# First modulation weight by columns in quarters, low output quarters on GpSimd, an early product in the second quarter of the passes

## The reference, cut to what matters

```python
mod = (silu(c) @ w_mod + b_mod)                    # c: (1, 1024), w_mod: (1024, 6144)
sh1, sc1, g1, sh2, sc2, g2 = split(mod, 6)         # and the same of c_ctx
h  = rms_norm(x, norm1_g) * (1 + sc1) + sh1        # 1024 tokens
hc = rms_norm(ctx, norm1_g) * (1 + csc1) + csh1    # 256 tokens
q_a, k_a, v_a, q_b, k_b, v_b = split(h @ w_in)     # and of hc
o_a, o_b = window_attention(...), neighbourhood_attention(...)
x = x + g1 * (concat(rms_norm(o_a), rms_norm(o_b)) @ w_out)
x = x + g2 * ((silu(h2 @ w_gate) * (h2 @ w_up)) @ w_down)
# second block: y @ w_in_2, a gMLP and a gated linear attention mixer, w_out_2, then
f = square(relu(rms_norm(h, pre_ff_g) @ w_ff1)) @ w_ff2
```

## Time and profile before

| | |
|---|---|
| median of 3 runs | 2323.98 us (2321.5 to 2325.11) |
| profiled execution | 2320.64 us, its span 2318.9 us |
| PE busy | 2263.4 us (98%) |
| PEld busy | 1867.7 us (81%) |
| DVE busy | 1481.0 us (64%) |
| ACT busy | 1020.7 us (44%) |
| POOL busy | 365.6 us (16%) |
| mean granted clock of PE | 0.995 |

### The profile page before, as it was taken

The page is one execution under the profiler, slowest core; times in us unless marked ns, Lnnn a source line. Parts: engine busy times, 40 slices in busy tenths (PEclk is TensorE's granted clock), DMA queues, the critical chain, the costliest instruction groups (busy, mean ns, idle before and its releaser), DMA issues. The chain is left out here.

```text
span 2318.9 us, 34643 instructions
## 1 busy us (share of the span) xinstructions
PE 2263.4 (98%) x12884; PEld 1867.7 (81%) x12884; DVE 1481.0 (64%) x2408; ACT 1020.7 (44%) x2030; POOL 365.6 (16%) x342
## 2 busy tenths in 40 slices
PE   6999999999999999999999999999989999999998
PEld 3878778878878888888888976988878888888886
DVE  3533278776687777776689423234587777666687
ACT  3523178875343232323444433233355555444444
POOL 2493400154340000000001000131240000000011
PEclk9999999999999999999999999999999999999999
DMA  8142350015213232326654411113224444666553
GB/s 321 37 147 90 120 120 28 2 47 167 107 58 124 89 126 86 119 87 214 212 186 142 148 37 46 38 38 143 103 96 150 150 152 148 239 202 217 173 168 123
DMA packets 156129, 289.73 MB, mean 125 GB/s; under 512 B 11998, under 2 KB 59820, under 8 KB 152764
## 3 DMA queue, kind: packets, MB, share of 16 engines
q1 hardware_dynamic: 155964, 287.52, 36.8%
HBM read 219.04 MB, written 70.62 MB: 125 GB/s over the span
## 5 line engine op out<-in xcount | busy, mean ns | idle before, releaser
L2270 PE MATMUL ps<-ff_b_hi,ff_a_hi 128*128 128x512 f32 x448 | 174.5, 390 | 0.2 <-DVE ff_b_lo L2258 0.2
L2271 PE MATMUL ps<-ff_b_lo,ff_a_hi 128*128 128x512 f32 x448 | 174.3, 389 | 0.0
L2272 PE MATMUL ps<-ff_b_hi,ff_a_lo 128*128 128x512 f32 x448 | 174.3, 389 | 0.0
L2231 ACT ACTIVATE ff_a_hi<-ff_a_raw 128x512 fp32r<-128x512 f32 x112 | 70.7, 631 | 157.3 <-PE ps L2272 149.9
L1964 ACT ACTIVATE swiglu_w_hi<-swiglu_stage 128x512 fp32r<-128x512 f32 x110 | 69.0, 630 | 160.6 <-PE ps L2023 151.9
L2021 PE MATMUL ps<-ht_hi,swiglu_w_hi 128*128 128x512 f32 x352 | 137.8, 392 | 0.6 <-DVE ht_lo L1916 0.6
L2022 PE MATMUL ps<-ht_lo,swiglu_w_hi 128*128 128x512 f32 x352 | 137.0, 389 | 0.0
L2023 PE MATMUL ps<-ht_hi,swiglu_w_lo 128*128 128x512 f32 x352 | 137.0, 389 | 0.0
L2256 DVE TENSOR_TENSOR ff_a_lo<-ff_a_raw,ff_a_hi 128x512 fp32r<-128x512 f32 x112 | 80.6, 719 | 83.2 <-ACT ff_a_hi L2231 83.2
L453 DVE TENSOR_TENSOR w_lo<-stage,w_hi 128x2048 fp32r<-128x2048 f32 x23 | 58.9, 2562 | 112.6 <-ACT w_hi L449 112.4
L2270 PE MATMUL ps<-swiglu_b_hi,swiglu_a_hi 128*128 128x512 f32 x308 | 120.3, 391 | 0.4 <-DVE swiglu_b_lo L2258 0.4
(11 more groups left out here) (466 smaller groups left out, 6479.9 us busy)
## 6 DMA issues: line engine op xcount, KB each, us to landing
ff_a_raw<-ff_act_dram SPq DMA_DIRECT2D x112, 256.0 KB, 2.7
swiglu_a_raw<-swiglu_act_dram SPq DMA_DIRECT2D x77, 256.0 KB, 2.8
stage<-w_in SPq DMA_DIRECT2D x18, 1024.0 KB, 5.2
stage<-w_mod SPq DMA_DIRECT2D x16, 1024.0 KB, 4.6
ff_stage<-w_ff SPq DMA_DIRECT2D x16, 1024.0 KB, 5.4
ff_act_dram<-ff_act_sums SPq DMA_DIRECT2D x16, 1024.0 KB, 4.3
ff_act_dram<-ff_acts SPq DMA_DIRECT2D x16, 768.0 KB, 5.6
swiglu_stage<-w_gate SPq DMA_DIRECT2D x11, 1024.0 KB, 6.3
```

The costliest lines, as they stand in the source:

```text
L2231: act.activation(a_hi[r][:, :], a_raw[s % LOOK][:, :], ACT.Copy).then_inc(f.a2_hi, 1)
L2270: pe.matmul(bank, a_hi[r][:, cols], b_hi[r][:, :], start=first, stop=False)
L2271: pe.matmul(bank, a_hi[r][:, cols], b_lo[r][:, :], start=False, stop=False)
L2272: return pe.matmul(bank, a_lo[r][:, cols], b_hi[r][:, :], start=False, stop=last)
```

## The change

1. SP loads the 2048 columns in four quarters by columns (`mod_quarter` on SP): 256 columns of the shift and 256 of the scale, two loads of 1 MiB with pieces of 1 KB, all 1024 rows. Behind quarter 0 come the constants, tiles 0 and 1 and part 0 of `w_in`; then quarter 1, part 1, quarter 2, tiles 2 and 3, quarter 3. PE sums a quarter with 8 matmuls 2x512: rows j and j+4 go to the same one of four partition groups (`mod_quarter_pe`), and four small matmuls with `row_picks` add up and turn the four groups. Each quarter gives the columns of two chunks (`mod_quarter_dve`), from which ACT and DVE make these two chunks (`quarter_hi_of_pair`, `quarter_y_of_pair`, `half_lo_of_pair`). In PE's order the sums of quarters 1 to 3 stand inside the products of the first pair, and the turn of the first pair behind quarter 0.
2. The low quarters of `w_out` in attention are made by POOL (`quarter_low`), at the end of its tables; the last two of the four units in which ACT makes the high quarters move; `rows_a` is cut in two, tiles 0 to 4 ahead of the last `table_inner` and 5 to 7 behind.
3. In both passes the product P1 of the second quarter stands ahead of P4 of the first, with the turn of the last block after its second step, and the turns use the banks differently so that bank 5 is free for it.

The core of the diff (the new functions whole):

```diff
+        def mod_quarter_pe(pe, g):
+
+            pe.wait_ge(modw_in[g], 32)
+            for j in range(KT):
+                at_row = 32 * (j % 4)
+                sums = ps[at_row:at_row + 2, 3, :].rearrange("p (s n) -> p s n", s=2)
+                mm = pe.matmul(sums, cond[:, :, j], mod_w[:, :, j, 256 * g:256 * g + 256], start=(j < 4), stop=(j >= 4))
+            mm.then_inc(part_done, 1)
+            pe.wait_ge(part_evac, g + 1)
+            for e in range(4):
+                pe.matmul(ps[:, 2, 8 * e + 2 * g:8 * e + 2 * g + 2], mod_part[:, e * P:(e + 1) * P], row_picks[:, :],
+                          start=True, stop=True).then_inc(mod_done, 1)
+
+        def mod_quarter_dve(dve, g):
+
+            dve.wait_ge(part_done, g + 1)
+            dve.tensor_copy(mod_part[:, :], ps[:, 3, :]).then_inc(part_evac, 1)
+            dve.wait_ge(mod_done, 4 * g + 4)
+            if g == 0:
+                dve.wait_ge(vec_ready, 1)
+            for w in range(2):
+                dve.tensor_tensor(mod_cols[:, w, :].rearrange("p (s k) -> p s k", s=2)[:, :, 2 * g:2 * g + 2],
+                                  ps[:, 2, 0:32].rearrange("p (s h g w) -> p w g s h", s=2, h=2, w=2)[:, w, g],
+                                  vec_cols[:, 0:16].rearrange("p (s k) -> p s k", s=2)[:, :, 2 * g:2 * g + 2], ALU.add).then_inc(cols_done, 1)
+            dve.wait_ge(cols_done, 3 * g + 2)
+            dve.scalar_tensor_tensor(out=gain_cols[:, :, 2 * g:2 * g + 2], in0=mod_cols[:, :, KT + 2 * g:KT + 2 * g + 2], scalar=1.0,
+                                     in1=bcast(vec_cols[:, 16 + 2 * g:18 + 2 * g], 1, 2), op0=ALU.add, op1=ALU.mult).then_inc(cols_done, 1)
...
+        def quarter_hi_of_pair(act, g):
+
+            act.wait_ge(tr_done, 2)
+            act.wait_ge(cols_done, 3 * g + 3)
+            for k in (2 * g, 2 * g + 1):
+                source, gain, shift = pair_source(0, k)
+                act.activation(pair_tokens(0, 0)[:, k, :], source, ACT.Identity, bias=shift, scale=gain).then_inc(chunk_hi, 1)
...
+        def quarter_y_of_pair(dve, g):
+
+            dve.wait_ge(cols_done, 3 * g + 3)
+            dve.wait_ge(chunk_hi, 2 * g + 2)
+            for k in (2 * g, 2 * g + 1):
+                source, gain, shift = pair_source(0, k)
+                made = dve.tensor_scalar(pair_y(0)[:, k, :], source, gain, shift, ALU.mult, ALU.add)
+            if g % 2:
+                made.then_inc(y_made, 1)
...
+        def half_lo_of_pair(dve, half):
+
+            ks = slice(4 * half, 4 * half + 4)
+            dve.wait_ge(y_made, half + 1)
+            dve.wait_ge(chunk_hi, 4 * half + 4)
+            dve.tensor_tensor(pair_tokens(0, 1)[:, ks, :], pair_y(0)[:, ks, :], pair_tokens(0, 0)[:, ks, :].bitcast(F32),
+                              ALU.subtract).then_inc(tl_done, 1)
...
-                    if i == 0:
-                        pe.wait_ge(w_lo_done, P_X + part + 1)
                     wh, wl = piece_weights(0, part)
                     for k in range(4):
+                        if i == 0 and k % 2 == 0 and 2 * part + k // 2:
+                            mod_quarter_pe(pe, 2 * part + k // 2)
+                        if i == 0 and k == 0:
+                            pe.wait_ge(w_lo_done, P_X + part + 1)
...
-            pair_hi(act, 0)
+            quarter_hi_of_pair(act, 0)
+            quarter_hi_of_pair(act, 1)
             split_hi(act, 1, 1)
+            quarter_hi_of_pair(act, 2)
             sums_of_pair(act, 1)
+            quarter_hi_of_pair(act, 3)
...
-        QUARTER_AT = [unit(B, 2, 3), unit(B, 2, 5), unit(B, 2, 7), unit(B, 3, 0)]
+        QUARTER_AT = [unit(B, 2, 3), unit(B, 2, 5), unit(B, 3, 0), unit(B, 3, 1)]
...
-                if u in QUARTER_AT:
-                    quarter_dve(dve, QUARTER_AT.index(u))
...
-                    rows_a(pool)
+                    roots_a(pool)
+                    rows_a(pool, range(5))
                 for j in range(2):
                     table_inner(pool, i, j)
+            rows_a(pool, range(5, NT))
+            for q in range(4):
+                quarter_low(pool, q)
...
-        def quarter_dve(dve, q):
+        def quarter_low(pool, q):
 
             if q == 3:
-                dve.wait_ge(w_hi_done, P_O + 1)
+                pool.wait_ge(w_hi_done, P_O + 1)
             else:
-                dve.wait_ge(quarter_hi, q + 1)
-            low = dve.tensor_tensor(quarter(out_lo0, q), quarter(out_raw, q), quarter(out_hi0, q).bitcast(F32), ALU.subtract)
+                pool.wait_ge(quarter_hi, q + 1)
+            low = pool.tensor_tensor(quarter(out_lo0, q), quarter(out_raw, q), quarter(out_hi0, q).bitcast(F32), ALU.subtract)
             if q == 3:
                 low.then_inc(w_lo_done, 1)
...
+                dve.wait_ge(w_lo_done, P_O + 1)
...
+            def mod_quarter(g):
+                for side in range(2):
+                    first = D * side + 256 * g
+                    sp.dma_start(mod_w[:, side, :, 256 * g:256 * g + 256],
+                                 t["w_mod"][0].rearrange("(p k) n -> p k n", k=KT)[:, :, first:first + 256]).then_inc(modw_in[g], 16)
+
+            def x_rows(first):
+                for j in (first, first + 1):
+                    sp.dma_start(q_nat[:, j, :], t["x"][0, j * P:(j + 1) * P, :]).then_inc(x_in[j], 16)
+
+            mod_quarter(0)
+            sp.dma_start(ident[:, :], t["k_ident"]).then_inc(pe_consts_in, 16)
+            sp.dma_start(vec_rows[0:16, :], t["b_mod"][0, 0:2 * D].rearrange("(k n) -> k n", n=P)).then_inc(vec_in, 16)
+            sp.dma_start(vec_rows[16:24, :], t["norm1_g"][0].rearrange("(k n) -> k n", n=P)).then_inc(vec_in, 16)
+            x_rows(0)
+            load_weights(sp, P_X, x_piece(0, 0), in_piece(stage))
+            mod_quarter(1)
             load_weights(sp, P_X + 1, x_piece(0, 1))
+            mod_quarter(2)
+            x_rows(2)
+            mod_quarter(3)
...
+            pe.transpose(ps[:, 2, 32:56], vec_rows[0:24, :], ident[0:24, 0:24]).then_inc(vec_turned, 1)
+            mod_quarter_pe(pe, 0)
+            pair_turn(pe, 0, q_nat[:, 0:2, :])
             first_pe(pe)
...
+            dve.memset(ps[:, 3, :], 0.0).then_inc(banks_clear, 1)
+            dve.wait_ge(pe_consts_in, 16)
+            dve.tensor_reduce(row_picks[:, :], ident[:, :].rearrange("p (g r) -> p r g", r=32)[:, 0:2, :], AX_X, ALU.add).then_inc(banks_clear, 1)
...
+            dve.tensor_copy(vec_cols[:, :], ps[:, 2, 32:56]).then_inc(vec_ready, 1)
+            dve.wait_ge(banks_clear, 2)
+            mod_quarter_dve(dve, 0)
             for b in range(2):
                 root_tile(dve, b, T_X, q_nat[:, b, :])
+            quarter_y_of_pair(dve, 0)
             split_lo(dve, 0, 0)
...
+            mod_quarter_dve(dve, 1)
+            quarter_y_of_pair(dve, 1)
+            half_lo_of_pair(dve, 0)
+            split_lo(dve, 1, 1)
+            mod_quarter_dve(dve, 2)
+            quarter_y_of_pair(dve, 2)
+            for b in (2, 3):
+                root_tile(dve, b, T_X, q_nat[:, b, :])
+            mod_quarter_dve(dve, 3)
+            quarter_y_of_pair(dve, 3)
+            half_lo_of_pair(dve, 1)
...
-                return 4 + (e % 4 if e < 12 else (e - 12) % 3)
+                return 4 + (e % 4 if e < 12 else (0, 1, 2, 0, 2, 0, 2, 0)[e - 12])
...
+            def made_at(q, b):
+                return {(0, P4): 7, (1, P1): 6}.get((q, b), place_of(q, b))
...
-                    pe.wait_ge(f.lo7, f0.lo7 + 24)
+                    pe.wait_ge(f.lo7, f0.lo7 + (18 if b == P1 else 24))
...
-            f.turn_block(pe, 4, 3)
+            for k in f.product_steps(pe, 1, P1):
+                if k == 1:
+                    f.turn_block(pe, 4, 3)
             f.product(pe, 0, P4)
-            for q in range(1, f.Q):
+            for b in range(1, 7):
+                f.product(pe, 1, b)
+            for q in range(2, f.Q):
                 for b in range(7):
...
             f.weight_lo(dve, 0, P4)
+            f.weight_lo(dve, 1, P1)
             f.block_lo(dve, 4, 0)
-            f.weight_lo(dve, 1, P1)
```

More of the change, by code:

```diff
@@ L182, in program @@
         y_made, chunk_hi = early("y_made"), early("chunk_hi")
-        modw_in = [early(f"modw_in{j}") for j in range(8)]
+        modw_in = [early(f"modw_in{j}") for j in range(4)]
         ctx_landed = early("ctx_landed")
@@ L1455, in rows_a @@
             pool.wait_ge(on_in, 32)
-            for j in range(NT):
+        def rows_a(pool, tiles):
+            for j in tiles:
                 row = q_nat[:, j, 0:AW]
@@ L2034, in keep @@
             def keep(act, q):
[L2036 removed]
+                act.wait_ge(f.made, f0.made + made_at(q, P1) + 1)
                 if q:
```

62 lines of the change are left out of this document (9 added, 53 removed).

## The result

| | before | changed |
|---|---|---|
| median | 2324.95 us (7 runs, 2320.9 to 2331.94) | 2330.34 us (7 runs, 2326.81 to 2339.77) |
| span of the profiled execution | 2318.9 us | 2328.0 us |
| PE's mean granted clock | 0.995 | 0.993 |

The ratio is 1.0040, 95% interval 1.0025 to 1.0055: the changed kernel is slower by 0.4%, some 9 us. (The two medians lie only 5.4 us apart, the profiled executions 9.1. The forecast was 2324.6, a change of +0.6 us, with "within 0.2%" as the likeliest; the measured time lies inside the range, on the side of rival 1.

A forecast was written before the change was run, and what follows sets the result against it. TensorE, busy 98% of the span, was taken as the bound, leaving only 55.5 us idle or lower-clock time to change. Startup 7.5, attention −3.5 and passes −3.4 gave +0.6 on 2323.98: 2324.6 us, 8-in-10 range 2317 to 2331.5.

The forecast's parts named there:

- rival 1: Startup: half clock through all quarters, sums as well as products; startup +14.9, net +8.0, 2332 us; chance 0.27.
- part A: Startup with w_mod in quarters: more turnarounds and late low weights eat the earlier start; +7.5 us, between +5.5 and +9.6.
- a shift passes through whole: After the startup: TensorE work is a chain, so any shift of the second pair's first product reaches the end whole.
- part C: Both passes: an early product of 2.76 us covers PE's waits of 1.7 and 2.0; −3.4, bounds −2.5 and −3.7.
- Part B: Attention: low quarters moved from DVE to GpSimd remove PE's waits for `small`; −3.5 us, bounds −1.5 and −3.8.
- it would be wrong if: Signs: quarter 1 or 2 sums wait for loads, early products wait for weights, or time after 60 us changes elsewhere.
- The chain: Startup: three later quarters of 6.93 us each after the first product, second pair at 56.6 at upper clock, +5.5 us.
- Quarter 0: Startup: data there at 11, sums to 14.7, first product at 25.7 us, 10.3 earlier than before.
- The clock, where I chose: Startup turnarounds: +5.5 us if the upper clock holds, +9.6 if it falls in each; the middle, +7.5, was taken.
- The sign that I had named: Startup, 25 to 58 us: mean granted clock about 1.00 at +5.5, about 0.75 at +9.6, below 0.65 at +14.9.
- The faster one (loads bind): Startup: shorter chain, quarter 3's load at 38.8 binds; startup −1.5, net −8.4, 2315.6 us; 0.18 including cases up to +5.5.

The follow-up runs named there:

- `after_3`: The changed kernel executed a third time, unchanged; the second pair's first product stood at 59.75 us.
- `a_cal`: Startup's quarters alone on the kernel before, plus 16, 3 and 5 zero matmuls in PE's waits; 1.0017, 3.9 us slower than before.
- padded kernels: Kernel before with GpSimd low quarters and early product, plus 32 or 56 tiny zero matmuls in PE's waits for w_mod; 0.9986 and 0.9972.
- part A alone: Only the startup's half of the diff (quarters of the modulation weight) on the kernel before, executed twice; 1.0042, 9.8 us slower.
- `bc`: The change with the startup of before put back, keeping GpSimd low quarters and the early product; 0.9982, 4.2 us faster than before.
- `a_ahead`: Startup's quarters alone, next quarter's sums ahead of this one's products, DVE's low weights and columns earlier; 1.0042 against the kernel before.
- `a_lo_first`: Startup's quarters alone, with DVE's first low weights ahead of the values of chunks 0 and 1; 1.0029, 6.7 us slower than before.

## Why the prediction was wrong

The steps that failed are three terms of the sum. Along PE's path in the first profile: part A's startup +12.6 where the sum has +7.5; "a shift passes through whole", where another +2.7 came by 345 us; part C −1.8 where it has −3.4. Part B held (−4.0 for −3.5). The signs named as "it would be wrong if" came up too: time after 60 us changed at several other places.

**Part A, forecast +7.5, measured +7.1 to +12.6, five executions.** The chain was right: no quarter's load was waited for behind the first, and each quarter has two waits on PE for DVE and ACT. In `after_3` the later quarters are entered at 36.91, 46.81 and 54.22; the steps are 8.65, 9.9 and 7.4 us, where my terms give 8.6, 9.7 and 6.9. The 0.5 at the last is DVE's copy, which waited behind the root tiles of the second pair. Two terms failed.
- *Quarter 0.* I put the first product at 25.7; it was at 28.1 to 28.4 in four executions and at 26.70 in one. `row_picks`, which I put at no cost, waits for `ident` behind both loads, and PE's first work waits for it (12.3 us in the profile after), so the sums start at 12.46, not 11. The picks took 1.87 for 1.06 and the turn 3.68 for 1.91 to 2.60; that is the lower rate, since both fell to 1.07 and 1.97 with the fillers of `a_cal`. That makes even the executions with the best clock +7.1 and +8.6 in place of the +5.5 that I had for them.
- *The clock, where I chose.* I took the middle between "holds" and "falls", because 3.7 to 5.4 us of dense work lie ahead of each turnaround. In three of five executions it fell in two or three turnarounds, with up to 3.05 us for sums of 1.9 and 3.2 for the turn, both of which I had at the full rate in that case: +12.2 to +12.6, against +9.6. That is two thirds of the way to rival 1 (+14.9), to which I had given 0.27. The sign that I had named, the mean granted clock between 25 and 58 us (1.00 at +5.5, 0.75 at +9.6, below 0.65 at +14.9), does not tell the cases apart: it read 1.00 at +8.6, 0.92 at +7.1, and 0.79, 0.87 and 0.86 at +12.6, +12.5 and +12.2. The picture that rival 1 cited (the Trainium skill, TensorE: Matmul & The Clock Gate, "HAM oscillation"), every slice starting at half rate, is seen in part in these three; `after_3`, with the clock at 1.00 between 35 and 60 us and the same waits, shows that here it did not always happen. And I drew more from this place of the Trainium skill than it gives: its case has less work on a slice than waiting for the next, while a quarter here has 3.7 us of work or more against a turnaround of 3.2.

**What passes on, forecast whole.** It did not pass on whole, it grew. Behind the startup come 0.5 us for a load of w_mod near 295 us, and 1.5 to 2.2 us more of the stall for instructions (with some matmuls at half clock beside it): together +2.7 in the first profile of the changed kernel and +3.7 to +4.2 in the other four of this startup. No part of my sum looked for PE's own instruction stream; the row was there as 0.66 us of "issue" at 325 us. The padded kernels show what sets its size: where in the burst PE runs dry. Part A moves both against each other, by a few us. That the whole ended at +9.1 after all is in part luck: behind 700 us the first profile has +1.6 near 1413, −2.9 near 1622 and +0.9 near 1700 us, none of them in the sum.

**Part B, forecast −3.5: measured −4.0.** The waits for `small` in the four units are gone (1.6 of 6.1 is left, near 310 us, where before has it too). The gain is above my bound of −3.8 by 0.2, and part A alone, without B, already shows 0.15 over the same units. POOL's last quarter:

```profile
523.60 2.52 POOL L1458 TENSOR_TENSOR out_lo<-out_raw,out_hi 128x512 fp32r<-128x512 f32 x2
...
529.96 1.28 POOL L1458 TENSOR_TENSOR out_lo<-out_raw,out_hi 128x512 fp32r<-128x512 f32 x1 [2.40 <-ACT out_hi L1449]
533.73 0.19 POOL L1528 TENSOR_SCALAR msq<-sumsq 128x1 f32<-128x1 f32 x1 [2.50 <-ACT junk L1494]
```

The last one ends at 531.24, 2.5 us before the next work of POOL; less the 11.4 us by which PE is later there that is 519.8, where I had 519.

**Part C, forecast −3.4, bounds −2.5 and −3.7: measured −1.25 and −0.6.** The two waits of the earlier trace rows are 0.1 each. But in the ff pass a new one stands 20 us later:

```profile
1747.42 0.47 PE L2086 MATMUL ps<-ht_hi,ff_w_hi 128*128 128x512 f32 x1 [1.01 <-DVE ff_acts L2127]
```

The turn of the last block now comes behind two steps of the early product, so in `bc` its low half is made 0.9 us later against the shift of the kernel there (2.8). PE gains 1.86 at the turn, but DVE and ACT go on only 1.9 us earlier than in before where PE is 4.65 earlier, and 20 us later PE has to wait 1.0 for a joined bank and gives back 1.27. The missing term is "what is late next", and it is the chain of DVE and ACT. In the swiglu pass the gain was 0.4 short of the 1.67; the late turn may be why, but no run shows it.

**Rivals.** The faster one (loads bind) failed as argued: in the order of the change PE came to no quarter before it was loaded. The loads of 1 KB pieces ran at 367 GB/s at a DMA share of 1.08 (20 to 40 us in `a_ahead`), against 410 in the same stretch of before; the rule of the Trainium skill (DMA: Bandwidth & Descriptors, Specifications) that pieces from 512 B on go at line rate is off by 10% here. They bind once PE's order is better, as `a_ahead` shows.

**What stays open.** A and B with C measured apart sum to +5.6 us (1.0042 and 0.9982); together they were +9.3 and +11.2. The intervals are some 3 us each side, and part A's spread over executions is 5 us, so this may be chance. But all six profiles with B and C have a spell at half clock near 1413 us, worth 1.5 to 3.2 us, which neither profile of before and neither of part A alone has; `a_ahead` and `a_lo_first` have it too, so no part is shown as its cause. Near 1622 us all changed kernels gain 1 to 3 us. For 1.6 of it the first profile of before is the reason, which was at half clock for a while there, where the changed ones were not:

```profile
1622.00:1627.00 5.00, 4.82 (x14) 3.83 (x15) 0.13 (x1) 0.18 (x1) 0.00 (x0) 0.66 0.96 331
```

The rest goes with the wait for `w_lo`: 2.3 and 2.5 us in the profiles of before, 1.0 in those of the changed kernel, but 2.2 in `bc` and 2.6 in `a_cal`. I have no cause for it.

## What to carry to other kernels

A load that is cut in pieces so that work can start earlier pays its turnaround once for each piece: before cutting, count the turnarounds that stand in the consumer's queue with nothing beside them (here four of 3.2 us for a start 8 us earlier), and then look for work to put beside them. The next piece's sums ahead of this piece's products brought this startup forward in one profile (56.3 for 58.2 to 63.7), but not the kernel, since the loads were then late. Where the matrix engine goes from one long wait to several short ones, take the lower clock as the case to plan for, and more than once if one execution shows it and another does not. And after any gain upstream, follow the engines that feed the one you relieved: in the ff pass they were one microsecond behind.

## What the runs showed of the hardware

- PE can stand for want of instructions: 0.3 to 4.5 us in these profiles, when no 16 KB packet of them had come for 16 us beside loads that moved 130 GB/s at a DMA share of 1.02. Adding 128 or 224 instructions elsewhere made this stall 4.48 or 0.31 us in place of 1.21.
- Packets of 2 KB took 0.29 us each in one burst of loads and 0.08 in another a few us earlier; the size of a packet alone does not give its rate.
- The same startup took 5.5 us more or less from one execution to another (58.22 to 63.74 for the second pair), with the same waits and another granted clock; the one of before, with one long turnaround, agreed within 0.7 us in two executions.
- Matmuls of zeros in the waits held the rate up: PE's idle 32 and 20% of the two stretches from 20 to 60 us fell to almost nothing, and with the smaller number of them the second pair came 2.7 to 8.3 us earlier than without. A float32 matmul of 128x128 took 0.24 us at full clock, where a transpose of that size took 0.12; the first try, sized by the transpose, cost what it gained.
- A stretch that prints a clock of 1.00 at the start of a profile may have no record of it: eight products took 3.7 us there, and 1.9 to 2.0 later.
